# Attention scores in three PSUM banks, and three half-tiles of the output projection multiplied during the last attention rows

## The chip, the cores and the metric

The kernel runs on one core of a Trainium2 chip. The time is device microseconds of one launch; lower is better. Below, PE is TensorE (matrix products and transposes), DVE is VectorE, ACT is ScalarE, POOL is GpSimd and SP is SyncE, which issues most of the DMAs. Each engine works through its own instruction stream in order and waits for the others by semaphores.

## What is computed

One encoder layer over 512 tokens of width 1024 and a final normalisation. The part that the change touches is the mixer: a convolution branch and an attention branch, each 512 wide, are put side by side and multiplied by one output matrix. The cut reference:

```
def mixer(xn, w_in, b_in, conv_w, conv_b, ln_g, ln_b, rpb, w_out, b_out):
    proj = jnp.einsum("bsd,de->bse", xn, w_in) + b_in
    glu_a, glu_g, q, k, v = jnp.split(proj, [...], axis=-1)
    conv_out = conformer_conv(glu_a, glu_g, conv_w, conv_b, ln_g, ln_b)   # 31 taps, LayerNorm, SiLU
    na_out = neighbourhood_attention(q, k, v, rpb)                        # 8 heads, 4 column blocks
    mixed = jnp.concatenate([conv_out, na_out], axis=-1)
    return jnp.einsum("bse,ed->bsd", mixed, w_out) + b_out

h = x + mixer(rmsnorm(x), ...)
h = h + moe(rmsnorm(h), ...)          # top 4 of 32 experts
out = rmsnorm(h, g_final)
```

## The kernel before

The 512 tokens are four tiles of 128 (`NQ` = 4). A product in near-float32 precision is made from three float32r products: high by high, high by low, low by high, where "low" is what rounding left over. So every operand is first copied to its high part (ACT) and its low part is made by a subtraction (DVE).

**The attention rows.** There are 32 steps (`NS`), one for each tile n and head. Step i is a small pipeline over the engines. PE multiplies q by k for two steps at once (`qk_pair`, L1814); DVE adds the position table and finds the row's maximum (`scores`, L1233); ACT takes the exponential (`exp_row`, L807); PE transposes the row (`transpose_p`, L1824); ACT copies it back (`pT_out`, L755); PE multiplies it by v (`pv`, L1835, all heads of a tile into bank 7). After eight heads DVE divides by the row sums (`normalise`, L1262 and L1267), PE transposes the result in bank 5 (`transpose_o`, L1845), ACT and DVE make `attn_high` (L827) and `attn_low` (L1248). The scores lie in PSUM banks 0 to 3 in rotation, and `qk_pair(i + 4)` is issued inside step i.

**The convolution** shares these steps. DVE makes two of the 31 x 4 taps (L1176) in each of the first 18 steps. Then comes LayerNorm over channels: PE's mean (L1896, steps 14 to 18, bank 5), DVE's centring (L1288, steps 19 to 22, out of bank 5), ACT's squares (L852), PE's variance (L1904, steps 29 to 32, bank 0), ACT's square root (L855), DVE's reciprocals (L1294) and scaling (L1297), ACT's SiLU (L858) and `conv_high` (L863), DVE's `conv_low` (L1302).

**The output projection.** `project_attn(n)` is 24 products of 128x512 for tile n: two halves of the output, each of 12 products (L1856 to L1858). `project_conv(n)` adds 24 more into the same two banks (L1869 to L1871). The order on PE at the end of the rows is: variance in steps 29 to 32, `project_attn(1)` in step 33, `transpose_o(3)` in step 34, then `project_attn` of tiles 0, 2 and 3, then `project_conv(0)`, `project_conv(1)`, `turn_xn2(0)` (L1926, transposes of the normalised tile for the router), `project_conv(2)` and so on. `wout_low_part` (L1256) makes the low parts of the output matrix on DVE: four of them in steps 24, 26, 28 and 30, four after the scaling.

**What follows on ACT and DVE.** After `conv_high` ACT's queue issues seven small DMAs: router bias, router weights, a norm row and four bias rows (L867 to L872). ACT then splits weight piece 0 (L879), waits for the bias rows, splits them (L884, L885) and splits piece 1. DVE makes the low parts of these (L1327, L1332, L1334) and only then adds the projection to the residual h (`residual`, L1239). ACT's sum of squares (L890), POOL's power (L595) and DVE's `norm2` (L1309) end in `turn_xn2(0)`. POOL adds `b_out` to h by four accumulating DMAs (L611); DVE waited for these just before the first residual.

## Time and profile before

| | us |
|---|---|
| median of 3 runs | 1321.04 (1320.98 to 1321.33) |
| the profiled execution, whole | 1320.23 |
| its span in the trace | 1318.5 |
| attention steps on PE, `transpose_p(0)` to the end of the variance | 141.0 to 200.1 |
| products of `project_attn` | 200.1 to 222.1 |
| `project_conv`, router and transposes | 222.1 to 255.5 |
| experts and the combination | 277 to the end |

The span is cut into stages by the first and last instruction of a line. A row of a timeline names the start, the duration, the engine, the line, what is written and read, and in square brackets how long the engine had been idle before and on what. A row of the chain is a piece of the path that ended last: its start, its length, the engine, what it writes and the line; "issue" is time in which the trace shows no releaser. In a table by stretch the columns are the stretch, its length, each engine's busy time with the number of instructions, the granted PE clock (1.00 is 2.4 GHz, 0.50 is 1.2 GHz), the DMA engines' share and the GB/s.

### The profile page before, as it was taken

The page shows a single profiled execution, that of the slowest core. Times are in us where ns is not written, and L with a number is a line of the kernel's source. Part 1 is how long each engine was busy: PE and PEld are TensorE (multiplying, and loading weights), DVE is VectorE, ACT ScalarE, POOL GpSimd, SP SyncE. Part 2 cuts the span into 40 slices and gives each one's busy share as a digit, 9 for nine tenths or more (in the row PEclk, how much of TensorE's full clock was granted, in tenths as well). Part 3 has the DMA queues.
Part 4 walks back from the last instruction along what each step waited for, and adds up shares of the span by engine and source line. Part 5 has one row for each costly group of instructions (what it writes and reads, how often), then busy time and mean ns, then how long its engine had stood idle before and what let it go on. Part 6 is the DMA issues. An engine that isn't in the chain of part 4 may idle for free.

```text
span 1318.5 us, 17626 instructions
## 1 busy us (share of the span) xinstructions
PE 1262.6 (96%) x5723; PEld 1002.1 (76%) x5723; DVE 1217.9 (92%) x1022; ACT 963.5 (73%) x786; POOL 308.7 (23%) x245
## 2 busy tenths in 40 slices
PE   4999889889999999999999999999999999999986
PEld 3887668777877878787778778788787877878763
DVE  6899966699999999999999999999999999999995
ACT  4241755358797979788888888897979797979841
POOL 5001000101131313141304132332323231313232
PEclk8999889989999999999999999999999999999999
DMA  8925791599999999999999999999999999999984
GB/s 282 388 82 144 283 355 37 205 330 409 393 420 406 423 408 411 413 412 421 412 413 411 420 409 421 412 419 411 421 410 422 411 423 412 420 410 407 420 342 164
DMA packets 89962, 481.60 MB, mean 365 GB/s; under 512 B 11018, under 2 KB 11317, under 8 KB 40775
## 3 DMA queue, kind: packets, MB, share of 16 engines
q1 hardware_dynamic: 77742, 448.89, 84.5%
q0 software_dynamic: 10400, 27.14, 6.0%
q10 hardware_dynamic: 1784, 5.14, 1.2%
q8 instruction: 18, 0.29, 0.1%
q14 instruction: 18, 0.14, 0.0%
HBM read 447.46 MB, written 41.66 MB: 371 GB/s over the span
## 4 chain that ended last, share of the span: by engine, by line
PE 78%; DVE 14%; ACT 3%; issue 3%; DMA 2%; DVEq 0%; SPq 0%; ACTq 0%; POOL 0%
PE pair L2000 13%; PE pair L2001 12%; PE pair L2002 12%; PE pair L2016 11%; PE pair L2017 11%; DVE area_m L1176 4%; DVE w_low L1327 3%; PE pair L1987 2%; PE pair L2014 2%; PE pair L1980 2%; PE pair L2023 2%; PE pair L2035 2%; PE pair L1777 1%; PE pair L1778 1%; PE pair L1779 1%
## 5 line engine op out<-in xcount | busy, mean ns | idle before, releaser
L1327 DVE TENSOR_TENSOR w_low<-w_raw,w_high 128x2048 fp32r<-128x2048 f32 x380 | 835.9, 2241 | 26.8 <-ACT w_high L879 24.9
L879 ACT CAST w_high<-w_raw 128x2048 fp32r<-128x2048 f32 x380 | 700.9, 1876 | 156.1 <-PE pair L2002 124.6
L2016 PE MATMUL pair<-w_high,xS 128*128 128x512 f32 x480 | 195.6, 407 | 0.1
L2000 PE MATMUL pair<-w_high,xT_high 128*128 128x512 f32 x480 | 192.2, 400 | 1.6 <-DVE w_low L1327 1.6
L2001 PE MATMUL pair<-w_low,xT_high 128*128 128x512 f32 x480 | 187.9, 391 | 0.0
L2017 PE MATMUL pair<-w_low,xS 128*128 128x512 f32 x480 | 187.4, 390 | 0.0
L2002 PE MATMUL pair<-w_high,xT_low 128*128 128x512 f32 x480 | 187.3, 390 | 0.0
L659 POOL DMA_INDIRECT y_rows<-area_m,place_now x30 | 103.6, 3455 | 44.0 <-issue 38.6
L2000 PEld LDWEIGHTS pair<-w_high,xT_high 128*128 128x128 f32 x480 | 90.1, 188 | 31.0 <-issue 7.7
L2016 PEld LDWEIGHTS pair<-w_high,xS 128*128 128x128 f32 x480 | 90.2, 188 | 23.3 <-issue 4.2
L2017 PEld LDWEIGHTS pair<-w_low,xS 128*128 128x128 f32 x480 | 90.2, 188 | 21.8 <-issue 3.8
L2000 PE MATMUL pair<-w_high,hT_high 128*128 128x512 f32 x256 | 102.2, 399 | 3.3 <-DVE w_low L1327 3.3
L2002 PEld LDWEIGHTS pair<-w_high,xT_low 128*128 128x128 f32 x480 | 90.1, 188 | 19.6
L638 POOL CAST sel_in<-is_expert 128x128 fp32r (+1 forms) x16 | 46.9, 2932 | 242.1 <-PE pair L2017 242.1
L2001 PEld LDWEIGHTS pair<-w_low,xT_high 128*128 128x128 f32 x480 | 90.2, 188 | 17.4
L2001 PE MATMUL pair<-w_low,hT_high 128*128 128x512 f32 x256 | 100.3, 392 | 0.0
L2002 PE MATMUL pair<-w_high,hT_low 128*128 128x512 f32 x256 | 100.3, 392 | 0.0
L2016 PE MATMUL pair<-w_high,hS 128*128 128x512 f32 x240 | 95.0, 396 | 0.0
L2017 PE MATMUL pair<-w_low,hS 128*128 128x512 f32 x240 | 93.5, 390 | 0.0
L1176 DVE SCALAR_TENSOR_TENSOR area_m<-area_u,convT,area_m 128x512 f32<-128x512 f32 x120 | 83.8, 750 | 0.4
L625 POOL COPY tok_now<-tok_tab 128x1 int32 (+1 forms) x31 | 24.3, 784 | 187.2 <-PE pair L1980 85.5
L2000 PEld LDWEIGHTS pair<-w_high,hT_high 128*128 128x128 f32 x256 | 48.4, 189 | 14.8 <-issue 3.8
(373 smaller groups left out, 1865.3 us busy)
## 6 DMA issues: line engine op xcount, KB each, us to landing
w_raw<-in_w_gate SPq DMA_DIRECT2D x128, 1024.0 KB, 9.5
w_raw<-in_w_up SPq DMA_DIRECT2D x128, 1024.0 KB, 10.9
w_raw<-in_w_down SPq DMA_DIRECT2D x128, 1024.0 KB, 10.1
y_rows<-area_a SPq DMA_DIRECT2D x1, 15360.0 KB, 53.2
ring<-in_w_in SPq DMA_DIRECT2D x5, 2048.0 KB, 18.9
y_rows<-area_t SPq DMA_DIRECT2D x1, 9216.0 KB, 30.0
ring<-in_w_out SPq DMA_DIRECT2D x2, 2048.0 KB, 8.1
h<-in_x SPq DMA_DIRECT2D x4, 512.0 KB, 9.1
```

Of the source, the lines that this page charges most:

```text
L638: g.tensor_copy(sel_in[:, :], is_expert[:, bass.ds(e, 1)].to_broadcast([P, CAP])).then_inc(sel_in_ready, 1)
L659: g.indirect_dma_start(out=y_rows, out_offset=bass.IndirectOffsetOnAxis(ap=place_now[0:CAP - first_row, 0:1], axis=0), in_=y_sb[first_row: ...
L879: s.copy(w_high[:, i % HIGH_RING, raw:], w_raw[i][:, raw:]).then_inc(high_ready, 1)
L1176: v.scalar_tensor_tensor(mixedT[:, c, :], u_pad[:, c, k:k + SEQ], convT[:, k * CC + c:k * CC + c + 1], mixedT[:, c, :], ALU.mult, ALU.add) ...
L1327: v.tensor_tensor(w_low[i][:, raw:], w_raw[i][:, raw:], w_high[:, i % HIGH_RING, raw:].bitcast(F32), ALU.subtract).then_inc(low_ready, 1)
L1980: last = t.transpose(bank[6 + k // 4][:, (k % 4) * CAP:(k % 4 + 1) * CAP], xg[0:CAP, k::KD], ident[0:CAP, 0:CAP])
L1987: last = t.transpose(bank[6 + k // 4][:, (k % 4) * CAP:(k % 4 + 1) * CAP], h_tok[:, k::KD], ident[0:CAP, 0:CAP])
L2000: t.matmul(to[half], tok_high, hi, start=(opens and kk == 0), stop=False)
L2001: t.matmul(to[half], tok_high, lo, start=False, stop=False)
L2002: last = t.matmul(to[half], tok_low, hi, start=False, stop=(k == KD - 1))
L2016: t.matmul(to[half], rows, w_high[:, i % HIGH_RING, cols], start=(opens and kk == 0), stop=False)
L2017: last = t.matmul(to[half], rows, w_low[i][:, cols], start=False, stop=(k == KD - 1))
```

## The change

It does the following.

- Scores rotate through banks 0 to 2. `qk_pair(i + 2)` is issued at the start of step i, ahead of `transpose_p(i)`, and waits for the scores of step i. `qk_pair(2)`, which stood ahead of `project_v(3)`, now follows it.
- Bank 3 holds three half-tiles of the attention projection, one after another: (tile 0, half 1), (tile 0, half 0), (tile 1, half 1). Each has 12 products, three in each of the steps 20 to 23, 25 to 28 and 30 to 33 (`project_early`). DVE adds each to h (`add_early`) in its steps 24, 29 and 34. `project_attn(0)` and the second half of `project_attn(1)` go; `project_conv` opens the three banks itself.
- `wout_low_part` 0 to 3 move to DVE's steps 18, 19, 23, 24. The variance moves to steps 30 to 33 and to bank 5; so `transpose_o(3)` waits for the square root, and the variance for `attn_low` of tile 2.
- DVE makes the reciprocals in step 34, and the scaling in step 35 ahead of `attn_low_part(3)`, which came between them. The wait for `b_out` moves ahead of the attention steps. ACT waits for three `attn_projected` instead of four.

The diff, shortened:

```diff
 TAP_STEPS = 18
+S_BANKS, ATTN_BANK = 3, 3
+EARLY = ((0, 1), (0, 0), (1, 1))
+EARLY_AT = (20, 25, 30)
 CENTRE_AT, SQUARE_AT, TURN_AT = 19, 20, 23
-MEAN_OF, VAR_OF = {14: 0, 15: 1, 17: 2, 18: 3}, {29: 0, 30: 1, 31: 2, 32: 3}
+MEAN_OF, VAR_OF = {14: 0, 15: 1, 17: 2, 18: 3}, {30: 0, 31: 1, 32: 2, 33: 3}
 next_tap, last_tap = [0] * CC, [0] * CC
...
         v_out(n)
-    for i in range(3):
+    for i in range(2):
         exp_row(i)
...
     for i in range(1, NS + 7):
-        if 3 <= i < NS:
+        if 2 <= i < NS:
             exp_row(i)
...
             wout_high_part((i - 4) // 2)
+        if i == NS + 1:
+            act.wait_ge(var_done, 1)
+            s.activation(ln_rs, bank[5][:, :], ACT.Sqrt, bias=eps_col[:, :]).then_inc(std_ready, 1)
         n = turned_at(i, 2)
...
             s.activation(sq[:, c, :], mixedT[:, c, :], ACT.Square).then_inc(squared, 1)
-        if i == NS:
-            act.wait_ge(var_done, 1)
-            s.activation(ln_rs, bank[0][:, :], ACT.Sqrt, bias=eps_col[:, :]).then_inc(std_ready, 1)
     for c in range(CC):
...
-    act.wait_ge(attn_projected, NQ)
+    act.wait_ge(attn_projected, NQ - 1)
     high_part(1, 0, 1)
...
             dve.wait_ge(exp_ready, i - 2)
-        v.tensor_tensor_reduce(out=S_sb[:, i % 3, :], in0=bank[i % 4][:, 0:KEYS], in1=table_of(n, hd),
+        v.tensor_tensor_reduce(out=S_sb[:, i % 3, :], in0=bank[i % S_BANKS][:, 0:KEYS], in1=table_of(n, hd),
                                scale=1.0, scalar=3.0e38, op0=ALU.add, op1=ALU.min,
...
-    WOUT_AT = {24: 0, 26: 1, 28: 2, 30: 3}
+    WOUT_AT = {18: 0, 19: 1, 23: 2, 24: 3}
+
+    def add_early(i):
+        n, half = EARLY[i]
+        dve.wait_ge(attn_early, i + 1)
+        v.tensor_tensor(h[:, n, half * HALF:(half + 1) * HALF], h[:, n, half * HALF:(half + 1) * HALF],
+                        bank[ATTN_BANK][:, :], ALU.add).then_inc(attn_added, 1)
+
+    dve.wait_ge(bout_added, 16 * NQ)
     for i in range(NS + 6):
...
             wout_low_part(WOUT_AT[i])
-        if i == NS + 3:
+        if i - 4 in EARLY_AT:
+            add_early(EARLY_AT.index(i - 4))
+        if i == NS + 2:
             dve.wait_ge(std_ready, 1)
...
                 v.reciprocal(ln_rs[:, q * P:(q + 1) * P], ln_rs[:, q * P:(q + 1) * P]).then_inc(ln_rs_ready, 1)
-    dve.wait_ge(ln_rs_ready, 4)
-    for c in range(CC):
-        v.tensor_tensor(mixedT[:, c, :], mixedT[:, c, :], ln_rs, ALU.mult).then_inc(ln_scaled, 1)
+        if i == NS + 3:
+            dve.wait_ge(ln_rs_ready, 4)
+            for c in range(CC):
+                v.tensor_tensor(mixedT[:, c, :], mixedT[:, c, :], ln_rs, ALU.mult).then_inc(ln_scaled, 1)
     for p in range(4, 8):
...
     dve.wait_ge(router_loaded, 32)
-    dve.wait_ge(bout_added, 16 * NQ)
     residual(0, 0)
...
         n = steps[i][0]
-        if i >= 4:
-            pe.wait_ge(s_ready, i - 2)
+        if i >= 2:
+            pe.wait_ge(s_ready, i - 1)
         spans = ((0, n * P, 192), (192, n * P - 64, 64)) if 0 < n < NQ - 1 else ((0, (n - n % 2) * P, KEYS),)
...
                 p0, hd = b * HEAD_DIM, steps[i + b][1]
-                last = t.matmul(bank[(i + b) % 4][:, o:o + w], qT[p0:p0 + HEAD_DIM, hd // 2, n * P:(n + 1) * P],
+                last = t.matmul(bank[(i + b) % S_BANKS][:, o:o + w], qT[p0:p0 + HEAD_DIM, hd // 2, n * P:(n + 1) * P],
                                 kT[p0:p0 + HEAD_DIM, hd // 2, key:key + w], start=True, stop=True)
...
             pe.wait_ge(centred, CC)
+        if n == NQ - 1:
+            pe.wait_ge(std_ready, 1)
         for c in range(4):
...
+    def attn_products(n, half, k, to, stop=False):
+        tokens = slice(n * P, (n + 1) * P)
+        t.matmul(to, attn_high[:, k, tokens], wout_high[half][:, 4 + k, :], start=(k == 0), stop=False)
+        t.matmul(to, attn_high[:, k, tokens], wout_low[half][:, 4 + k, :], start=False, stop=False)
+        return t.matmul(to, attn_low[:, k, tokens], wout_high[half][:, 4 + k, :], start=False, stop=stop)
+
+    def project_early(i, k):
+        n, half = EARLY[i]
+        if k == 0:
+            pe.wait_ge(wout_low_ready, 2 if i == 0 else 4)
+            pe.wait_ge(attn_low_ready, 4 * (n + 1))
+            if i:
+                pe.wait_ge(attn_added, i)
+        last = attn_products(n, half, k, bank[ATTN_BANK][:, :], stop=(k == 3))
+        if k == 3:
+            last.then_inc(attn_early, 1)
+
     def project_attn(n):
...
         pe.wait_ge(attn_low_ready, 4 * (n + 1))
-        tokens = slice(n * P, (n + 1) * P)
         for half in range(2):
-            to = bank[OUT_BANKS[n][half]][:, :]
-            for k in range(4):
-                t.matmul(to, attn_high[:, k, tokens], wout_high[half][:, 4 + k, :], start=(k == 0), stop=False)
-                t.matmul(to, attn_high[:, k, tokens], wout_low[half][:, 4 + k, :], start=False, stop=False)
-                last = t.matmul(to, attn_low[:, k, tokens], wout_high[half][:, 4 + k, :], start=False, stop=False)
+            if (n, half) not in EARLY:
+                for k in range(4):
+                    last = attn_products(n, half, k, bank[OUT_BANKS[n][half]][:, :])
         last.then_inc(attn_projected, 1)
...
             for k in range(CC):
-                t.matmul(to, conv_high[:, k, tokens], wout_high[half][:, k, :], start=False, stop=False)
+                t.matmul(to, conv_high[:, k, tokens], wout_high[half][:, k, :], start=(k == 0 and (n, half) in EARLY), stop=False)
                 t.matmul(to, conv_high[:, k, tokens], wout_low[half][:, k, :], start=False, stop=False)
...
     qk_pair(0)
-    qk_pair(2)
     project_v(NQ - 1)
...
     for i in range(NS + 5):
+        if i % 2 == 0 and i + 2 < NS:
+            qk_pair(i + 2)
         if i < NS:
             transpose_p(i)
-        if i % 2 == 0 and i + 4 < NS:
-            qk_pair(i + 4)
         if 1 <= i <= NS:
             pv(i - 1)
+        for e, at in enumerate(EARLY_AT):
+            if at <= i < at + 4:
+                project_early(e, i - at)
         n = turned_at(i, 0)
...
             if c == 0:
-                pe.wait_ge(s_ready, NS - 3)
-            last = t.matmul(bank[0][:, :], mean_w[:, :], sq[:, c, :], start=(c == 0), stop=(c == CC - 1))
+                pe.wait_ge(attn_low_ready, 12)
+            last = t.matmul(bank[5][:, :], mean_w[:, :], sq[:, c, :], start=(c == 0), stop=(c == CC - 1))
             if c == CC - 1:
...
             project_attn(1)
-    pe.wait_ge(std_ready, 1)
-    project_attn(0)
     pe.wait_ge(pT_ready, NS)
+    pe.wait_ge(attn_added, len(EARLY))
     project_attn(2)
```

## Rows read from the trace of the kernel before

**Rows 1.** The page: busy time, share of the span and number of instructions.

```profile
PE 1262.6 (96%) x5723; PEld 1002.1 (76%) x5723; DVE 1217.9 (92%) x1022; ACT 963.5 (73%) x786; POOL 308.7 (23%) x245
```

**Rows 2.** The chain that ended last, from variance to turn_xn2(0).

```profile
200.14 0.23 PE pair L1856
...
205.64 0.45 PE pair L1845 x4
...
207.29 1.12 DVE attn_low L1248 x4
...
209.05 4.81 ACT area_u L858 x4
...
216.67 4.99 DMA area_m<-in_b_gate
...
233.42 1.16 PE pair L1926 x8
```

**Rows 3.** Busy time of each engine by stretch.

```profile
172.10:199.60 27.50, 22.85 (x139) 16.55 (x137) 15.96 (x49) 18.09 (x57) 0.00 (x0) 0.94 0.83 316
...
156.00:169.60 13.60, 13.13 (x59) 10.91 (x58) 12.13 (x30) 7.96 (x23) 0.00 (x0) 0.50 1.05 410
...
190.10:193.50 3.40, 3.40 (x19) 3.40 (x18) 0.96 (x4) 1.98 (x8) 0.00 (x0) 0.50 1.04 394
...
199.60:222.10 22.50, 22.50 (x102) 18.42 (x101) 16.57 (x22) 12.24 (x16) 0.00 (x0) 1.00 0.20 54
```

**Rows 4.** The chain inside the attention rows: each PE operation, one exponential.

```profile
184.21 0.63 PE pair L1814 x4
...
193.16 0.63 ACT area_m L807 x2
...
195.67 0.25 PE pair L1824 x2
...
195.92 0.47 PE pair L1835 x4
...
196.40 0.92 PE pair L1904 x2
```

**Rows 5.** Timeline: DVE and PE held up in the attention rows.

```profile
172.10 0.69 DVE L1267 TENSOR_TENSOR area_a<-pair,area_m 128x512 f32<-128x512 f32 x1 [2.93 <-issue]
...
176.94 0.69 DVE L1288 TENSOR_TENSOR area_m<-area_m,pair 128x512 f32<-128x512 f32 x1 [3.46 <-PE pair L1896]
...
189.12 0.70 PE L1814 MATMUL pair<-area_k,area_q 64*128 64x256 f32 x4 [1.44 <-DVE area_m L1233]
```

**Rows 6.** Timeline: DVE's scores(2) and ACT's copy of the last v tile.

```profile
138.87 0.42 DVE L1233 CUSTOM_DVE_ANT_0 area_m<-pair,ring 128x256 f32<-128x256 f32 x1
...
139.93 0.58 ACT L814 COPY area_t<-pair 64x512 f32<-64x512 f32 x1
```

**Rows 7.** Timeline of POOL: the additions of b_out; the page: their landing.

```profile
111.35 3.67 POOL L611 DMA_DIRECT2D h<-in_b_out  x4 [85.46 <-DVE ring L1196]
...
h<-in_b_out POOLq DMA_DIRECT2D x4, 512.0 KB, 8.4
```

**Rows 8.** Timeline of ACT: square root, attn_high(3), SiLU's table load.

```profile
200.18 0.69 ACT L855 ACTIVATE area_a<-pair,small 128x512 f32<-128x512 f32 x1 [0.94 <-PE pair L1904]
...
206.12 1.14 ACT L827 ACTIVATE attn_high<-pair,colT 128x128 fp32r<-128x128 f32 x4 [5.25 <-PE pair L1845]
...
207.28 1.28 ACT L858 ACT_TABLE_LOAD   x1
```

**Rows 9.** Timeline of DVE: reciprocals, scaling, wout_low 4 to 7, conv_low.

```profile
200.90 3.39 DVE L1294 RECIPROCAL area_a<-area_a 128x128 f32<-128x128 f32 x4 [0.89 <-ACT area_a L855]
...
208.33 2.48 DVE L1297 TENSOR_TENSOR area_m<-area_m,area_a 128x512 f32<-128x512 f32 x4
...
210.74 4.62 DVE L1256 TENSOR_TENSOR wout_low<-ring,wout_high 128x1024 fp32r<-128x1024 f32 x4
...
215.28 2.48 DVE L1302 TENSOR_TENSOR conv_low<-area_u,conv_high 128x512 fp32r<-128x512 f32 x4
```

## Prediction made before the changed kernel was built

> **What bounds the kernel now.** I read the page's busy times first: PE is busy for 96% of the span, DVE for 92% [rows 1], so a stage may be set by either, and an average decides nothing. Then I read the chain of waits through the stage that is changed, from the end of the variance (V, 200.14) to `turn_xn2(0)` (233.42), from where PE runs the rest [rows 2]. The reader is to see where PE is missing. From V the chain goes through the 24 products of `project_attn(1)`, which end where `transpose_o(3)` begins (205.64), then over ACT's attn_high(3), DVE's attn_low(3) and scaling, ACT's SiLU, the landing of the bias rows, DVE's splits of weight pieces and biases, the residual and the norm, and back to PE [rows 2]. The 72 products of tiles 0, 2 and 3 and the 48 convolution products of tiles 0 and 1 lie beside it. PE was full in 199.6 to 222.1 [rows 3], but full of work that nobody on the chain waited for. Ahead of V the rows alternate between PE, ACT and DVE: in 172.1 to 199.6 PE is busy for 22.85 of 27.5 us [rows 3], and the gaps are waits on DVE or ACT, such as 1.44 us before the q by k of steps 30 and 31 [rows 5]. So there are two questions: when V comes, and how long it is from V to `turn_xn2(0)`, now 33.28 us.
>
> **Size of what moves.** The 24 products take 205.64 - 200.14 = 5.50 us, 0.229 each [rows 2]. Three halves are 36 products: 8.2 us of PE leave the stretch behind V and go into the steps ahead of it. The Trainium skill (TensorE: Matmul & The Clock Gate, Back-to-back issue gap) gives about 131 ns for a sustained 512-column product; by it the 36 would be an estimated 4.7 us and the rows would grow by 3.5 us less. The spacing in the trace is 0.229, so the trace disagrees with that figure for these float32r products.
>
> **Behind V: 3.2 us shorter.** Now only 12 products (2.75) stand between V and `transpose_o(3)`; this goes on to attn_high 0.48 later (205.64 to 206.12), attn_high(3) and the table load take 206.12 to 208.56 = 2.44 [rows 2, 8]: SiLU can start at V + 5.7. The other branch is shorter: root at V + 0.04, reciprocals at V + 0.76 for 3.39, one scaling of about 0.65, ready at V + 4.8 [rows 8, 9]. The third `add_early` (0.69, taken from the same shape in [rows 5]) stands ahead of the reciprocals, but its products end before the last variance product, so it fits into the 0.76. SiLU starts now at 209.05 = V + 8.9 [rows 2]; the chain gets 3.2 shorter. Everything behind SiLU is unchanged and in the same order: the seven DMA issues, the landing, the splits, the residual. So `turn_xn2(0)` comes at V + 30.1. What else could be late there? `conv_low`: scaling ends at V + 6.6, attn_low(3) 1.12, wout_low 4 to 7 4.62, conv_low 2.48 [rows 2, 9], so V + 14.8. PE has 60 products and four transposes, V + 14.2, starts the convolution at V + 14.8 and is through tile 1, 48 products or 11.0 later, at V + 25.8. It then waits 4.3 us for `turn_xn2(0)`. Of the 8.2 us taken from PE, most only lengthens that wait.
>
> **Ahead of V: 6.1 us longer.** No row shows these steps with extra products, so I bound it. Least: the 36 products fill all of PE's gaps in 172.1 to 199.6 (27.5 - 22.85 = 4.65) and the stretch at half clock, 190.1 to 193.5 at 0.50 [rows 3], disappears (half of 3.4 is 1.7): 8.2 - 6.35 = 1.9. Most: all 8.2, and a wait more. To choose, I walked the steps with the pieces of [rows 4]: two transposes 0.22 to 0.25, `pv` 0.43 to 0.47, `qk_pair` 0.65, a variance product pair 0.92, exponential 0.65 to 0.7, and `attn_low` 1.12 [rows 2], `wout_low` 1.15 (a quarter of [rows 9]), centring and adding 0.69 [rows 5], scores 0.42 [rows 6].
> - Steps 18 and 19: wout_low(0) fits before the mean (DVE waits 3.46 there [rows 5]). wout_low(1) stands behind the first centring and in front of scores(20), and `qk_pair(22)`, now in step 20, waits for scores(20): 1.1 late, to 178.9; PE idles 1.8.
> - Steps 20 to 25: PE does 0.69 more in each of four steps; in them it waits only 0.4 for ACT, which has the squares. The first add waits for step 23's product and holds scores(25), no loss so far, since PE is later. normalise(2) then holds `pv(24)`: PE reaches it at 188.4, gets it at 188.9.
> - Steps 26 to 28: attn_low(1) and (2) were late for PE before (the 1.44 us). Now PE has products in these steps and no longer waits; the 1.44 and the half clock go.
> - Steps 29 and 30: the second add waits on DVE for the last product of step 28 (196.1), and scores(30) is behind it: exponential and `transpose_p(30)` follow at 197.9, PE idle for 1.3.
> - Steps 30 to 33: each has transposes, `pv`, three early products and a variance product, 2.3 us a step, with nothing to wait for: V = 206.2.
>
> The tally: +8.2 for the products, -1.7 for the clock, -0.4 since PE's waits in the walk (1.8, 0.4, 0.5, 1.3 and bits) add up to 4.3 where the trace has 4.65: +6.1, near the upper end, because the early products stand in front of V in the same queue, four groups of three right beside the variance.
>
> **The first steps.** `qk_pair(2)` now waits for `project_v(3)` and, behind it, for ACT's two copies of the v tile (139.93 on, 0.58 each [rows 6]), so scores(2) goes from 138.87 to about 141.2, 2.4 us on DVE, which paces these steps with its taps. But DVE later stands 2.93 us before normalise(1) [rows 5], waiting for PE; the delay is covered and I cost it at nothing. Without that cover it would be 2.4. The wait for `b_out` costs nothing: issued by 115.0, landed some 8.4 us later [rows 7], and DVE begins its step 0 only two steps ahead of 138.87. The conv's opened banks add no instruction; the third add and the others (3 x 0.69) replace no residual. Waiting for three tiles on ACT is early anyway.
>
> **The clock behind V.** In the rows PE had been idle for 1.44 us and thinly used around it when its clock stood at 0.50 in 190.1 to 193.5 [rows 3, 5]. The new wait before `turn_xn2(0)` is three times as long, so I expect about one such stretch in `project_conv(2)`: 1.7 us, with PE on the chain there. The range of this is 0 to 3.4. The Trainium skill (TensorE: Matmul & The Clock Gate, What's actually happening) says the throttled state is the default and activity lifts it; it speaks for the products in the rows and against this wait, and the trace agrees at 190.1.
>
> **Sum.** +6.1 - 3.2 + 1.7 = +4.6 us. On the profiled execution's own time, 1320.23, that is 1324.8; the median lies 0.8 above that execution, so 1325.6. After 233.4 all is triggered by this stage's results, and I carry the shift to the end unchanged.
>
> **Rivals.**
> - *No clock loss* (the wait leaves PE at 2.4 GHz): +2.9, 1323.9. For it: the mean clock of 0.94 in 172.1 to 199.6 is accounted for by the one stretch of 3.4 us, so PE's other gaps there lowered nothing [rows 3]. Chance 0.20.
> - *The rows absorb the products*: PE fills nearly every gap, V moves by 1.9 to 4, total -1.4 to +2.5, 1319.6 to 1323.5. For it: 4.65 us of gaps; against it: the gaps are waits whose causes (normalise, the adds in front of scores) stay. Chance 0.18.
> - *Faster*: the rows absorb all, and with `qk_pair` at another place the stretch at half clock, 156.0 to 169.6 [rows 3], moves or ends sooner, so that PE no longer keeps normalise(1) waiting: up to the 2.93 us of DVE's wait [rows 5], so -1.4 - 2.9 = -4.3, 1316.7. It decides when V comes at 200.6 or earlier (+0.5 - 3.2 = -2.7). Chance 0.09.
> - *Slower than forecast*: an additional half-clock stretch or two in the rows, as the three banks take away PE's lead (1.8 idle in step 20), or the first 2.4 us not covered: +6.3 to +8, 1327.3 to 1329. Chance 0.08.
>
> **How the numbers follow.** Forecast with the clock loss, +3.5 to +6.2: 0.45. The line for "same" is 0.2%, 2.6 us, about what a measurement can tell from no change. Slower: 0.45 + 0.08 + 0.12 of the 0.20 = 0.65. Same: 0.18 + 0.08 = 0.26. Faster: 0.09. The range leaves out the faster case and the lowest third of the absorbed one below, and the top of the slow one above: 1320.8 to 1328.8.
>
> **What would show it.** V (the root's start) at about 206; SiLU's start 5.7 us behind it; a PE gap of some 4 us ahead of `turn_xn2(0)` at 236.3, and a clock of 0.50 behind it; scores(2) at 141.2; PE's gap in front of `transpose_p(30)`. The forecast is wrong if V comes before 203, or if the root-to-`turn_xn2(0)` stretch is not near 30.1.

## The result, and the profile after

| | before | after |
|---|---|---|
| median, us | 1321.14 (1320.40 to 1321.71, 6 runs) | 1329.01 (1326.14 to 1335.22, 6 runs) |
| the profiled execution, whole | 1320.23 | 1326.14 |
| its span in the trace | 1318.5 | 1324.4 |

The ratio is 1.0067, with an interval of 1.0050 to 1.0083: the change makes the kernel slower, by 7.9 us between the medians. Forecast were 1325.6 us and a range up to 1328.8, so the direction was right and the size too small. The profiled run is the quickest of its six: 5.9 us above the profiled run of before, where 4.6 were forecast. So the first trace explains a good part of the miss, but not all of it, and the spread has to be explained too.

The page of after, beside [rows 1]:

```profile
PE 1262.2 (95%) x5723; PEld 1000.5 (76%) x5723; DVE 1220.4 (92%) x1025; ACT 963.9 (73%) x786; POOL 308.8 (23%) x245
```

As many PE instructions, PE as long at work, three DVE instructions more: nothing was saved or added but the three additions. What changed is order, and the page can't show that. Below, "the root" is ACT's square root behind the variance, the V of the forecast, and "the first centring" is DVE's first subtraction of the mean, in step 19. The chain that ended last, from `transpose_o(3)` to `turn_xn2(0)`, answers to [rows 2] (start, length, engine, what is written, line):

```profile
210.22 0.45 PE pair L1862 x4
...
211.86 1.28 ACT L863
...
213.15 4.76 ACT area_u L863 x4
...
220.73 4.70 DMA area_m<-in_b_gate
...
237.18 1.97 PE pair L1958 x8
```

The same stations, in the same order. ACT's timeline answers to [rows 8] (start, duration, engine, line, what, and in brackets the idle time before):

```profile
207.49 0.69 ACT L853 ACTIVATE area_a<-pair,small 128x512 f32<-128x512 f32 x1 [3.89 <-PE pair L1937]
210.70 1.14 ACT L832 ACTIVATE attn_high<-pair,colT 128x128 fp32r<-128x128 f32 x4 [2.52 <-PE pair L1862]
```

The root starts 7.3 us later (207.49 for 200.18) and SiLU 5.66 behind it instead of 8.87. `turn_xn2(0)` comes 3.8 later. DVE's timeline shows the delayed scores(2) and the three additions, beside [rows 5] and [rows 6]:

```profile
141.05 0.42 DVE L1238 CUSTOM_DVE_ANT_0 area_m<-pair,ring 128x256 f32<-128x256 f32 x1 [2.46 <-PE pair L1829]
...
171.35 0.69 DVE L1272 TENSOR_TENSOR area_a<-pair,area_m 128x512 f32<-128x512 f32 x1
...
177.77 0.69 DVE L1301 TENSOR_TENSOR area_m<-area_m,pair 128x512 f32<-128x512 f32 x1 [3.91 <-PE pair L1929]
...
179.51 0.42 DVE L1238 CUSTOM_DVE_ANT_0 area_m<-pair,area_t 128x256 f32<-128x256 f32 x1
...
187.19 0.69 DVE L1282 TENSOR_TENSOR h<-h,pair 128x512 f32<-128x512 f32 x1 [1.27 <-PE pair L1869]
...
197.42 0.69 DVE L1282 TENSOR_TENSOR h<-h,pair 128x512 f32<-128x512 f32 x1 [0.71 <-PE pair L1869]
```

PE's timeline has the waits of steps 20, 25, 30 and behind the convolution, and in the two last lines two products issued behind the transposes, 0.42 apart instead of 0.23:

```profile
179.99 0.76 PE L1829 MATMUL pair<-area_k,area_q 64*128 64x192 f32 x8 [1.65 <-DVE area_m L1238]
...
189.92 0.63 PE L1850 MATMUL pair<-area_v,area_a 128*128 128x64 f32 x4 [0.57 <-DVE area_a L1272]
...
199.14 0.44 PE L1839 MATMUL pair<-ident,area_m 128*128 128x128 f32 x2 [1.14 <-ACT area_m L812]
...
237.18 1.97 PE L1958 MATMUL pair<-ident,area_a 128*128 128x128 f32 x8 [3.79 <-DVE area_a L1325]
...
239.38 0.63 PE L1901 MATMUL pair<-wout_low,conv_high 128*128 128x512 f32 x1
239.80 0.63 PE L1902 MATMUL pair<-wout_high,conv_low 128*128 128x512 f32 x1
```

And the stretches of PE, beside [rows 3]. The columns are the stretch, its length, PE's busy time with its instructions, the granted clock, the DMA share and the GB/s. The first is from DVE's first centring (step 19) to the root:

```profile
177.77:207.49 29.72, 26.36 (x159) 1.00 0.54 207
172.00:175.50 3.50, 3.31 (x10) 0.54 1.05 408
233.40:237.20 3.80, 0.02 (x1) 0.99 0.00 0
237.60:241.00 3.40, 3.40 (x14) 0.56 0.38 154
```

The same stretch in the trace of before, from first centring to root:

```profile
176.94:200.18 23.24, 19.29 (x115) 0.93 0.76 290
```

This is the cleanest number of the case: 29.72 - 23.24 = 6.5 us more between the same two points, with PE 7.1 us busier at the better clock, and idle for 3.4 instead of 4.0.

**More than one trace.** Since the times spread, the changed kernel and the one before were profiled again, unedited. Columns: starts of the first centring, the root, `norm2` of tile 0 and the last addition to h; then how much later than in the first trace of before the first expert steps and the last ones come.

| trace | time | centring | root | norm2(0) | last h | experts begin | end |
|---|---|---|---|---|---|---|---|
| before | 1320.23 | 176.94 | 200.18 | 232.08 | 246.46 | 0 | 0 |
| before_look | 1320.54 | 177.67 | 201.00 | 232.44 | 246.84 | +0.4 | +0.5 |
| after | 1326.14 | 177.77 | 207.49 | 235.84 | 251.76 | +5.3 | +5.8 |
| after_again | 1327.79 | 179.02 | 208.76 | 237.35 | 253.32 | +7.0 | +7.5 |
| after_third | 1334.48 | 177.57 | 207.30 | 235.19 | 251.18 | +6.4 | +14.0 |
| after_look4 | 1326.00 | 177.03 | 206.74 | 234.72 | 250.66 | +5.3 | +5.8 |
| after_look5 | 1325.67 | 177.19 | 206.91 | 235.37 | 251.32 | +5.0 | +5.3 |
| after_look6 | 1330.19 | 178.08 | 207.81 | 235.78 | 251.75 | +6.4 | +9.9 |

Centring to root is 29.71 to 29.74 in all six, and 23.24 and 23.33 in before. What differs is where the first centring lies, and what comes behind 252.

The rows do not begin at the same time in every trace, so the first steps are better measured from DVE's first scores, scores(0). Before and after:

```profile
135.53 0.41 DVE L1233 CUSTOM_DVE_ANT_0 area_m<-pair,ring 128x256 f32<-128x256 f32 x1
```

```profile
135.15 0.44 DVE L1238 CUSTOM_DVE_ANT_0 area_m<-pair,ring 128x256 f32<-128x256 f32 x1
```

From here the first centring comes 41.41 and 41.91 us later in the two traces of before, and 41.80 to 43.23 later in the six of after (median 42.6): the first steps take some 0.9 more. Scores(0) itself lies 0.3 earlier in after by the medians (135.34 for 135.65). Nothing ahead of it was changed but the place of the wait for `b_out`, which had landed by then [rows 7]; this earlier start hides a part of the cost in the columns above.

### The profile page after: what moved, and what is told of

Read it like the earlier page. It is cut to its first block, busy times and chain, and to the rows that moved or that the text cites. A ratio compares the mean times of both kernels' runs of the same rounds, so it can differ in the third digit from the quotient of the medians.

```text
span 1324.4 us, 17631 instructions
## 1 busy us (share of the span) xinstructions
PE 1262.2 (95%) x5723; PEld 1000.5 (76%) x5723; DVE 1220.4 (92%) x1025; ACT 963.9 (73%) x786; POOL 308.8 (23%) x245
## 4 chain that ended last, share of the span: by engine, by line
PE 81%; DVE 11%; issue 3%; ACT 2%; DMA 2%; SPq 1%; DVEq 0%; ACTq 0%; POOL 0%
PE pair L2032 13%; PE pair L2033 12%; PE pair L2034 12%; PE pair L2048 11%; PE pair L2049 11%; DVE w_low L1343 3%; DVE area_m L1181 2%; PE pair L2019 2%; PE pair L2046 2%; PE pair L2012 2%; PE pair L1792 2%; PE pair L2055 2%; PE pair L1794 2%; PE pair L1793 2%; PE pair L2067 1%
## 5 line engine op out<-in xcount | busy, mean ns | idle before, releaser
L2048 PEld LDWEIGHTS pair<-w_high,xS 128*128 128x128 f32 x480 | 90.2, 188 | 23.3 <-issue 4.2
```

The costliest lines, as they stand in the source:

```text
L2048: t.matmul(to[half], rows, w_high[:, i % HIGH_RING, cols], start=(opens and kk == 0), stop=False)
```

## Experiments

Two theories. The first is that of the forecast: the early products cost nearly full price ahead of the root, and buy only what hung on `transpose_o(3)` behind it. The second: the three banks and the steps moved with them cost the time, and the products nearly nothing. First, the number of early half-tiles was varied, with all other parts of the change kept.

**No early half-tiles (dose0), and two of three (dose2).** The first gives all 24 products of tile 0 back to the tail, behind the root's wait, and the second half of tile 1 to step 33 (ACT waits for four `attn_projected` again):

```diff
-EARLY = ((0, 1), (0, 0), (1, 1))
-EARLY_AT = (20, 25, 30)
+EARLY = ()
+EARLY_AT = ()
...
+    project_attn(0)
     pe.wait_ge(pT_ready, NS)
-    pe.wait_ge(attn_added, len(EARLY))
```

> The changed kernel with no half moved: three banks, moved steps, all 96 attention products behind the rows. Theory 1 (the products cost their own 8.2 us in the rows, the rotation costs little): the root starts at 200 to 202, turn_xn2(0) follows 33 us later, time within 2 us of before. Theory 2 (the loss ahead of the root comes from three banks and the lost lead of q by k): the root starts at 205 or later, as in the changed kernel, and the time is 6 us or more above before.

```diff
-EARLY = ((0, 1), (0, 0), (1, 1))
-EARLY_AT = (20, 25, 30)
+EARLY = ((0, 1), (0, 0))
+EARLY_AT = (20, 25)
```

> Only the two halves of tile 0 are moved; the half of tile 1 stays behind the rows. Theory 1: the root starts 2.7 to 4 us earlier than in the changed kernel, at 203.5 to 204.7; the stretch to turn_xn2(0) is some 33 us, since transpose_o(3) stands behind 24 products again; turn_xn2(0) at about 237, time about as the changed kernel. Theory 2: the root at 207 as in the changed kernel, turn_xn2(0) at 240, 3 us slower than the changed kernel.

> The kernel with no half moved once more, for a second trace of the same program. If the spread comes from PE's half-clock stretches in the rows: the root moves by 1.5 us or more against the first trace (203.3) together with the length at 0.50 between 170 and 200. If it comes from the experts: the root stays and the shift against before changes behind 290.

Measured: dose0 1323.2 us (1318.8 to 1331.7, 11 runs), ratio 1.0021 [1.0003, 1.0038]; dose2 1327.1 (1325.31 to 1333.6, 6 runs), ratio 1.0056 [1.0039, 1.0074]. The median of dose0 lies 2.5 us above before's, where the first theory had at most 2. The root of dose2, 205.54, lies between what the two theories had (203.5 to 204.7, and 207). The second profile of the first kernel (dose0_again, 1320.94) has no half clock in the rows behind 171, so three traces can be compared at full clock. First centring to root with no, two and three early half-tiles (dose0_again, dose2, after_again):

```profile
178.64:201.08 22.44, 18.51 (x123) 1.00 0.71 270
```

```profile
178.59:205.54 26.95, 23.59 (x147) 1.00 0.58 221
```

```profile
179.02:208.76 29.74, 26.38 (x159) 1.00 0.52 197
```

24 products lengthen the rows by 4.51 us, the next 12 by 2.79: 0.188 and 0.233 each, 7.30 for all 36, or 0.203. PE's idle time in the stretch falls only from 3.93 to 3.36. The first theory holds. The Trainium skill (TensorE: Matmul & The Clock Gate, Back-to-back issue gap) has about 131 ns for a sustained product of 512 columns; by it the 36 would have cost an estimated 4.7 us, and what was measured is 7.30. The second theory falls as the main cause: with three banks, the delayed scores(2) and all moved steps, but no early products, the root of dose0_again comes at 201.08, where before has 200.18 and 201.00. A smaller cost is there, though: by the ratios (1.0021 for 1.0067) the other edits make up about a third of the loss in time. Before runs 3.4 us of this stretch at half clock, and dose0_again none. If that is worth half its length, 1.7, centring to root should be 21.6 (23.3 - 1.7), and it is 22.44: the edits other than the products cost some 0.9. That "half its length" is an assumption; what is measured is that they and the clock together make this stretch 0.9 shorter. (These doses rest on one trace each; the stretch repeats within 0.1 us where a kernel has several at the same clock.)

The first profile of dose0 shows the exception. There the root comes at 203.32, with this stretch in the rows:

```profile
181.00:189.00 8.00, 7.94 (x42) 0.57 1.04 398
```

So without early products the same program has the half clock in the rows in one execution and not in the other, and that is worth about 2 us (24.48 from centring to root, for 22.44). This is 0.3 of the 6.9 us that the clock stood at half there (181.9 to 188.8), and not half: by this rate before's 3.4 us were worth 1.0, and the other edits cost only 0.1 to 0.2. The split between the two stays open.

**Removing the products and nothing else (before_less).** The kernel before, with the 36 products left out; those parts of the attention projection are missing in its output, the convolution opens the three banks, and ACT waits for three `attn_projected`. Its output is wrong by that, and the routing of the tokens too, so only what lies ahead of the router is compared:

```diff
+LEFT_OUT = ((0, 1), (0, 0), (1, 1))
...
         for half in range(2):
+            if (n, half) in LEFT_OUT:
+                continue
...
-    project_attn(0)
```

> The kernel before with the 36 products of the three halves left out altogether (the output lacks their part, and the routing is of other values, so only the time up to turn_xn2(0) is read). Theory 1 (24 of the 36 never were on the chain): root at 200.2, SiLU 5.7 behind it, turn_xn2(0) at 229.5 to 230.5, 3.2 us earlier than before, PE idle about 4 us ahead of it. Rival (PE is the bound behind the root): turn_xn2(0) about 8 us earlier, at 225.5, PE without a gap.

Measured: 1318.11 us, one execution. Its trace, ACT and PE:

```profile
198.52 0.69 ACT L856 ACTIVATE area_a<-pair,small 128x512 f32<-128x512 f32 x1 [0.94 <-PE pair L1907]
...
204.65 4.80 ACT L859 ACTIVATE area_u<-area_m,colT 128x512 f32<-128x512 f32 x4 [0.49 <-DVE area_m L1298]
```

```profile
228.77 1.64 PE L1928 MATMUL pair<-ident,area_a 128*128 128x128 f32 x8 [4.18 <-DVE area_a L1310]
```

```profile
229.00:233.00 4.00, 4.00 (x16) 0.57 0.34 135
```

SiLU comes 6.13 behind the root (8.87 before), the norm of tile 0 28.91 behind it (227.43 - 198.52; before 31.90, and 31.44 in before_look): taking 8.2 us of PE away brings 2.5 to 3.0. Then PE waits 4.18 us for the transposes, its clock stands at 0.57 on the mean behind them, and from `norm2(0)` to the last addition to h it takes 15.97 us (243.40 - 227.43), where before has 14.38: 1.6 given back. Even with the products gone altogether this stretch, root to the last addition, gains 1.0 to 1.4 us (44.88 for 45.84 and 46.28); the rest of the 3.1 by which that addition is earlier than in before (243.40 for 246.46) lies ahead of the root, where nothing was changed (198.52 for 200.18). That bounds what a move of them alone could bring there, and shows that the half clock behind the wait does not need the three banks.

**The wait in front of the transposes (swap).** After, with `project_conv(2)` and `project_conv(3)` each moved ahead of the transposes, so that PE has work while the norm is made:

```diff
     project_conv(1)
+    project_conv(2)
     turn_xn2(0)
-    project_conv(2)
-    turn_xn2(1)
     project_conv(3)
+    turn_xn2(1)
```

> The changed kernel with project_conv(2) ahead of turn_xn2(0), and project_conv(3) ahead of turn_xn2(1); nothing ahead of V changes. Theory 1 (PE's wait there and the half clock behind it are part of the loss): 3 to 5.5 us faster than the changed kernel, at 1.00 clock through the convolution products, runs close together. Rival (the norm chain on ACT, POOL and DVE sets the router's start, PE's wait is harmless): within 1 us of the changed kernel, with the same spread.

Measured: 1324.65 us (1323.17 to 1329.52, 9 runs), ratio 1.0038 [1.0025, 1.0052]. PE does not wait in front of the transposes, and there is no half clock from 218 to 262:

```profile
178.46:208.20 29.74, 26.38 (x159) 1.00 0.54 206
218.00:262.00 44.00, 38.15 (x228) 1.00 0.47 171
```

The last addition to h (248.14) can't be compared, since the products in front of it now stand ahead of the transposes. The experts can: ACT's first copy into `xS` lies 2.1 later than in before, where the table has 5.0 to 7.0 for after, although the root (208.20) is not earlier. The two rows are of before and of swap:

```profile
299.12 0.58 ACT L983 CAST xS<-pair 128x512 fp32r<-128x512 f32 x1 [1.64 <-PE pair L1980]
```

```profile
301.21 0.58 ACT L988 CAST xS<-pair 128x512 fp32r<-128x512 f32 x1 [1.64 <-PE pair L2012]
```

So the wait and the clock behind it are a cause of their own, worth 2.9 to 4.9 us where the experts begin. In the time, the ratios are 1.0067 and 1.0038, 0.3% or some 4 us; but they are of two comparisons, and their intervals touch ([1.0050, 1.0083] and [1.0025, 1.0052]). The runs were expected to lie close together, and they don't. The rows' 29.74 stay, and the kernel remains slower than before.

**The landing of the bias rows (rows_early).** After, with ACT's seven small DMAs and the two waits that stand with them (named `small_rows` in the edit) moved ahead of the root's wait:

```diff
     if i == NS + 1:
+        small_rows()
         act.wait_ge(var_done, 1)
```

> The changed kernel with the seven small DMAs of ACT issued ahead of the root instead of behind SiLU. Theory 1 (behind the root the chain is SiLU, landing of the bias rows, splits): the root stays within 0.5 us of 207.4, residual(0,0) comes 3.3 us earlier, PE's gap ahead of turn_xn2(0) shrinks from 3.8 us to under 1, no half clock behind it, 4 to 6 us faster than the changed kernel, and its runs lie close together. Rival (the spread and the loss come from the clock in the rows or the experts): time and spread as in the changed kernel.

Measured: 1327.18 us (1323.43 to 1328.27, 6 runs), ratio 1.0043 [1.0031, 1.0055]. The timeline of ACT:

```profile
208.12 1.28 ACT L863 ACT_TABLE_LOAD   x1 [5.27 <-issue]
209.41 0.69 ACT L863 ACTIVATE area_a<-pair,small 128x512 f32<-128x512 f32 x1
```

The norm of tile 0 comes 25.00 behind the root (234.41 - 209.41), 3.3 sooner than in after. Of this 0.8 is only the lateness of the root, since SiLU now comes 4.87 behind it and not 5.66; the other 2.5 lie behind SiLU. But the issues run until 208.1 and the table load stands behind them, where in after it had been done since 203.6, so the root is late for another reason, at 209.41. The last addition to h is at 248.79. The DMA landing was thus on the chain, as the forecast had it, and moving it gives 2.5 us there. The expected 4 to 6 us in the time did not come: the root gave up 1.4 (centring to root 31.12 for 29.74), and stretches at half clock came up later in that trace, at 282, 661 and 1282. The last two:

```profile
661.00:665.00 4.00, 4.00 (x12) 0.57 0.99 405
1282.00:1286.00 4.00, 4.00 (x16) 0.57 0.96 343
```

**The moved steps one by one.** The kernel before with the new places of `wout_low_part` only (before_wout), with the new places of the variance only (before_var), and the changed kernel without early products on four banks with the old lead (dose0_four):

```diff
-WOUT_AT = {24: 0, 26: 1, 28: 2, 30: 3}
+WOUT_AT = {18: 0, 19: 1, 23: 2, 24: 3}
```

> The kernel before with only wout_low 0 to 3 in DVE's steps 18, 19, 23, 24. If these moves leave PE thinly used in steps 20 to 28 and so spread the times: runs 6 us apart or more, median 1 to 4 us above before. If the variance's place does it: within 1 us of before, runs within 3 us.

```diff
-MEAN_OF, VAR_OF = {14: 0, 15: 1, 17: 2, 18: 3}, {29: 0, 30: 1, 31: 2, 32: 3}
+MEAN_OF, VAR_OF = {14: 0, 15: 1, 17: 2, 18: 3}, {30: 0, 31: 1, 32: 2, 33: 3}
```

> The kernel before with only the variance one step later, steps 30 to 33, still in bank 0. If PE's 512-column variance products are what brings the clock back, a later start leaves room for more half clock: runs 6 us apart or more, median 1 to 4 us above before. Otherwise: within 1 us of before, runs within 3 us.

```diff
-S_BANKS, ATTN_BANK = 3, 3
+S_BANKS = 4
...
-        if i >= 2:
-            pe.wait_ge(s_ready, i - 1)
+        if i >= 4:
+            pe.wait_ge(s_ready, i - 2)
...
-        if i % 2 == 0 and i + 2 < NS:
-            qk_pair(i + 2)
         if i < NS:
             transpose_p(i)
+        if i % 2 == 0 and i + 4 < NS:
+            qk_pair(i + 4)
```

> The kernel with no half moved, but scores in four banks again and q by k issued four steps ahead, as before; the moved low parts, variance, root, scaling and b_out wait stay. Theory 1 (three banks cost little, some 2.5 us, and spread the times): the runs lie within 3 us as those of before, median within 1 us of before, root at 200 to 201.5. Rival (the moved steps around the variance are what costs and spreads): median 2 to 3 us above before, runs 8 us apart or more, as with three banks.

Measured: before_wout 1326.85 (1321.49 to 1333.17, 10 runs), ratio 1.0027 [1.0002, 1.0052]; before_var 1327.48 (1320.13 to 1329.45, 10 runs), ratio 1.0016 [0.9991, 1.0041], not settled, since on that chip before itself had 10 of 29 runs at 1326.5 to 1329.3 (see below on the gathers); dose0_four 1325.78 (1322.27 to 1331.22, 11 runs), ratio 1.0042 [1.0027, 1.0056]. First centring to root takes 26.16, 24.00 and 26.33 us, where before has 23.24. In before_wout:

```profile
176.84:203.00 26.16, 22.27 (x115) 0.80 0.68 259
189.20:199.30 10.10, 10.03 (x39) 0.51 0.48 181
```

In before the stretch of lower clock is only [rows 3]'s 3.4 us at 190.1; here it is some 10 and runs past the first variance products. The trace of dose0_four has it too, with the same length. So two kernels on four banks in which the low parts are made early, and in which nothing fills PE in steps 25 to 29, lose 3 us here; the early products of the change fill just these steps and after has no half clock there in any of six traces. That `wout_low_part` 2 and 3 in steps 23 and 24 are what thins PE out is argued from their place, not shown; and it can't be all, since dose0_again, on three banks, has the low parts early and no products in these steps, and its clock stays at 1.00 (22.44 us). The medians of dose0_four and before_wout lie 4.9 and 5.4 above before, more than was expected of either.

**The last two: the DMA issues and the swap on the kernel before (before_rows_swap).** The kernel before, with the seven DMAs issued right behind the root and the order of the swap:

> The kernel before with the seven small DMAs issued right behind the root, and project_conv(2) and (3) one place earlier on PE. Theory 1: behind the root PE is full in this kernel, so only its 0.5 us wait and short waits up to the router go: 0.5 to 1.5 us faster than before, root unchanged. Rival (the chain of bias rows sets the pace here too): 3 us faster or more.

Measured: 1322.79 (1321.0 to 1329.99, 12 runs), ratio 0.9995 [0.9974, 1.0016]; the expected 0.5 to 1.5 us did not come. The root is at 201.03, `norm2(0)` 30.58 behind it, the last addition to h at 248.26, which is later than in before, since the convolution of tile 2 now stands ahead of the transposes. There is no gain to see: where PE is not waiting in front of the transposes, there is nothing for the swap to fill.

**Where the spread comes from.** The changed kernel unedited:

> The changed kernel once more, for a second trace of the same program. Its median is 3 us above its first trace. Either the root is later than 207.5, by half-clock stretches in the rows, or the shift grows behind turn_xn2(0) or within the experts, by stretches at 0.50 that the first trace lacks.

> The changed kernel, a third trace. As for the second: each microsecond above the first trace's 1326.1 shows as a later root (stretches at 0.50 among steps 18 to 33), as half clock behind turn_xn2(0), or as growth in the experts. The root is 66.4 to 67.5 us behind scores(2) if no half clock falls in steps 20 to 33, and more if one does.

> The changed kernel, unedited, a fourth look. Theory (products at full price in the rows, the wait in front of the transposes behind them): root start at 207.3 to 209.4, SiLU 5.66 behind it, last addition to h 15.9 us behind norm2(0) with a half-clock stretch of 3.4 us at 237 to 241; time 1326 to 1328. Rival (what lifts the median over the first profiled run is the tail, not the rows): everything up to 262 as in the first trace, and 1 to 9 us more from late row gathers on POOL or half-clock stretches behind 1240.

> The changed kernel, unedited, a fifth look; as for the fourth. If the root is again 7.1 to 8.6 later than in the kernel before, with the half-clock stretch ahead of 172 at 7 to 28 us, the rows' own cost is a range of 1.5 us and not one number.

> The changed kernel, unedited, a sixth look; as for the fourth. A late gather (9.7 and 6.4 us to issue) in it would give +7 us at the end and about 1334.

> The kernel before, unedited, a second look: whether its root start (200.18) and its last addition to h (246.46) repeat. If they repeat within 0.5 us and its half-clock stretches ahead of 172 and at 190 too, the differences stand; if the stretch at 190 is missing, the root comes about 1.7 earlier and the products cost more than their 8.2. Time 1320 to 1322, or 1327 to 1329 with late gathers.

The times and marks are in the table of the first section. The roots of after_look4 (206.74) and after_look5 (206.91) are a little earlier than expected. The second trace of before repeats what the argument rests on, its half clock at 190 included (0.93 as in the first):

```profile
177.67:201.00 23.33, 19.30 (x115) 0.93 0.74 282
```

Behind the last addition to h, which lies 4.2 to 6.9 us later than in the first trace of before, the traces part in four places.

- At 285 to 289 after_third, after_look4 and after_look6 stand at half clock: +1.1 to +1.7 between the last addition and the experts. In these three the half clock during the router ended sooner, after 13.6 us (264.3 to 277.9 in after_look4) where the first trace of after and that of before have 17.0 (264.5 to 281.5, and 258.4 to 275.4).
- Near 662 PE waits for a split in every trace, 1.59 us in before and 1.95 in after: +0.4 (+0.3 to +0.5). In after_look6 a half clock follows, and it is +1.8.
- At 1285 to 1289 after_look6 stands at half clock once more, +1.6. It has none at 1271 to 1275, where the first trace of after has one of 3.4 us (before at 1265 to 1269): it came later here, not in addition. The trace of before_rows_swap, a kernel on four banks, has it late too, at 1279.8 to 1283.2.
- In after_third +7.1 come at the end, by another mechanism (below).

The lines of after_look6 for the first three:

```profile
285.00:289.00 4.00, 4.00 (x13) 0.57 0.67 262
664.00:668.00 4.00, 4.00 (x11) 0.57 0.98 400
1285.00:1289.00 4.00, 4.00 (x15) 0.57 0.95 332
```

The same places in the first trace of after, where the wait of 1.95 us at 662 is there but no half clock:

```profile
284.00:289.00 5.00, 5.00 (x32) 1.00 0.86 315
664.00:668.00 4.00, 4.00 (x18) 1.00 1.02 421
1285.00:1289.00 4.00, 4.00 (x12) 1.00 0.92 316
```

And POOL in after_third, where it gathers rows of `y_rows`:

```profile
1253.59 4.13 POOL L716 DMA_INDIRECT w_raw<-y_rows,slot_of_rank  x1 [8.38 <-PE pair L2049]
1258.02 9.70 POOL L716 DMA_INDIRECT w_raw<-y_rows,slot_of_rank  x1 [0.30 <-issue]
1268.03 6.43 POOL L716 DMA_INDIRECT w_raw<-y_rows,slot_of_rank  x1 [0.30 <-issue]
```

In before the same three:

```profile
1246.63 1.93 POOL L711 DMA_INDIRECT w_raw<-y_rows,slot_of_rank  x1 [8.38 <-PE pair L2017]
1248.87 1.90 POOL L711 DMA_INDIRECT w_raw<-y_rows,slot_of_rank  x1 [0.30 <-issue]
1251.07 0.94 POOL L711 DMA_INDIRECT w_raw<-y_rows,slot_of_rank  x1 [0.30 <-issue]
```

DVE waits for the third gather and PE for DVE, 5.90 us at 1288. The trace of before_var has the same (4.14, 9.70 and 6.43), and ends 7.7 us late with a root only 0.7 late. So the late gathers need nothing of this change; which executions have them is open. Both traces are of one chip, on which before_wout and before_rows_swap were traced without them.

## Why the forecast was right in direction and too small

**Behind the root: right.** Root to SiLU was to be 5.7 and is 5.66; the gain of 3.2 is 3.5 by the medians of the table (root to `norm2(0)` 28.2, before 31.7). The wait before `turn_xn2(0)` was to be 4.3 and is 3.79 at 237.18 (forecast 236.3), and the clock stands at half behind it, as forecast. Its price was put at 1.7, from 0 to 3.4: `norm2(0)` to the last addition takes 15.92 to 15.99 in the six traces, 14.38 and 14.40 in before, so 1.6. The rival without clock loss falls, and before_less shows both steps on the other kernel.

**Ahead of the root: right in kind, too small.** The forecast was +6.1 for the rows and nothing for the steps ahead of them. By the medians the root is 6.8 later; but from scores(0) to the root it is 72.3 us (71.51 to 72.97) where before has 64.65 and 65.24, so +7.4. Centring to root gives 6.4 of it (29.72 less 23.3), and the first steps the rest. The walk had the waits: step 20 1.65 (1.8 forecast) with scores(20) at 179.51 (178.9), `pv(24)` 0.57 (0.5), `transpose_p(30)` 1.14 (1.3). The products themselves cost a little less than their length, 7.30 by the doses for 8.2. The half clock at 190 went, as forecast: the stretch has a clock of 1.00 in all six traces. Whether that was worth the credited 1.7 is not shown (dose0's two traces speak for 1.0). If it was, the other edits cost some 0.9, and before_var shows one of them: the variance one step later, alone and with the half clock at 190 still there, makes centring to root 24.00 for 23.24. The walk had put that move at nothing. So the terms: forecast 8.2 - 1.7 - 0.4 = 6.1, measured 7.3 for the products and -0.9 for the clock and the other edits together, 6.4.

**The first steps: 0.9 us, forecast at nothing.** Scores(2) waited 2.46 (2.4 forecast) and the wait before `normalise(1)` (2.93 in [rows 5]) took up most of it, as written: after the delay DVE stands there 0 to 1.3 us. In the first trace of after nothing was lost up to there, 36.20 us from scores(0) to `normalise(1)` for 36.57 in before, and so it is in after_look5 and after_look6. But in these three a second, short half clock (172.3 to 175.7 in the first) falls in front of the mean, and `normalise(1)` to the first centring takes 6.42 us for 4.84. In the other three that takes 4.79, but scores(0) to `normalise(1)` takes 37.01 to 38.44. The longest is after_again, whose PE runs at half clock for all of this stretch:

```profile
143.00:171.00 28.00, 27.48 (x134) 0.51 1.04 403
```

In [rows 3] this was 13.6 us; in before_look it was 17.1, and the first centring came 0.5 later behind scores(0). In dose0_again it was 20.4, and its centring came at 178.64, late too. A run separates the rotation from the other edits: dose0_four, with four banks and the old lead, has 41.40 us from scores(0) to the first centring, and dose0 and dose0_again, with three, have 44.26 and 42.92. So the cost comes with the three banks and the delayed scores(2), and not with the moved steps. How much of it is the delay itself and how much the clock, whose stretches at half lie differently from trace to trace, is not separated.

**The stage's sum held, in part by luck.** Last addition to h by the medians: 251.5 less 246.65, +4.9 us, for +4.6. From scores(0) it is +5.4; the earlier start of the rows, which the change does not explain, made good some of what the first steps cost. The rival in which the rows absorb the products is out, as is the faster one.

**The step that failed is the last: "I carry the shift to the end unchanged", and with it the offset of 0.8 between profiled run and median.** The first steps, which it costed "at nothing" and which took 0.9, are the second, smaller one. The carried shift and the offset both took the rest of the program for a fixed length. The six traces end 5.3, 5.8, 5.8, 7.5, 9.9 and 14.0 later than before, from +4.2 to +6.9 at 252. By the medians of the six, +4.9 at the last addition becomes +5.85 where the experts begin and +6.65 at the end: 1.75 us came up in the part that the forecast held fixed. The six have a median time of 1327.0; the five executions of the first comparison that were not profiled have 1327.2 to 1335.2, and where their time went was not seen. The six times of the kernel before in that comparison and its two profiled ones lie within 1.5 us, so its trace gave no warning of this spread; the range should all the same have reached further up than the terms of one stage make it, since a shift can change the waits behind it (at 662 PE's is 1.59 and 1.56 us in before, and 1.90 to 1.96 in after).

What stays open, besides those five: why the half clock comes at 285, 662 and 1285 in some executions, and in neither trace of before (rows_early has all three, before_rows_swap the last). The waits ahead of it at 662 are 1.59 and 1.95 us, close to each other, and 1.95 is there with and without it.

## What to carry to other kernels

Work moved from a stage in which PE hides it into one whose gaps are waits of a pipeline is paid nearly in full (7.3 of 8.2 us here), and brings only what hung on it in its old place (3.5); price the two ends apart, and ask of each gap whether its cause stays. Removing the work from the old place altogether, as before_less did, bounds the gain in one run, and shows the next wait. When the moved work leaves PE dry for some microseconds on the critical chain, count the half clock behind it (1.6 us here), and when edits shift a long program, expect stray stretches of it further on.

## What the runs showed of the hardware

- The same program runs with the granted clock at half in different places: for 6.9 us from 155.2 and 3.4 from 172.3 in the first trace of after, for 27 up to 171 in after_again; at 181.9 to 188.8 in one trace of dose0 and not in the other. The Trainium skill (TensorE: Matmul & The Clock Gate, What's actually happening) says that the point at which the clock rises varies from run to run; these traces agree. One stretch was worth from 1.1 us to some 2 us of the kernel's time (at 285, and at 181.9 in dose0).
- An indirect gather of POOL took 0.94 to 1.93 us to issue in 16 of 18 traces; in after_third and before_var the first of three took 4.1 us and the next two 9.70 and 6.43. On the chip on which before_wout and before_var ran, 10 of 29 runs of the unchanged kernel took 1326.5 to 1329.3, the others 1318.5 to 1322.3; that these have the late gathers is a guess from the size (+7), since none of them was profiled.
- ACT loads the root's table ahead of its wait when nothing stands before it (done 3.9 us ahead of the root's start in after), and behind the DMA issues in rows_early, where its 1.28 us fell on the chain.
